# Cached values in earlier places, and the samples' softmax behind the prompt's first two logits steps

## The reference

```python
q, k, v, qi, ki, wi = split(x @ w_in)          # 16 heads of 64, 4 KV heads; 8 index heads
score = einsum(relu(qi . ki), wi) * IDX_SCALE  # every query against every visible key
_, idx = top_k(score, topk)                    # 128 keys (prompt), 256 keys (sample)
logits = q . k_sel * ATTN_SCALE + t5_bias      # only the kept keys
out = softmax(logits) @ v_sel                  # samples: K and V come from paged caches
y = LN(ALPHA * x + out @ w_out)                # then a squared-ReLU MLP, LN, layer 1, MLP
```

## Time and profile before

| what | us |
|---|---|
| median of three runs | 1305.32 |
| lowest and highest run | 1297.4, 1305.51 |
| the profiled execution | 1300.45 |
| its span in the trace | 1298.8 |
| TensorE busy, share of the span | 1215.7, 94% |
| VectorE, ScalarE, GpSimd busy | 708.2, 473.8, 102.0 |
| DMA moved | 129.99 MB |

### The profile page before, as it was taken

How to read it: one execution, slowest core, us unless ns; L and a number is a source line. 1 busy time by engine, 2 the same in 40 slices (tenths; PEclk the granted TensorE clock), 3 DMA queues, 4 the chain that set the end, 5 groups by cost and what they waited for, 6 DMA issues and landing times.

```text
span 1298.8 us, 25590 instructions
## 1 busy us (share of the span) xinstructions
PE 1215.7 (94%) x9573; PEld 1113.3 (86%) x9573; DVE 708.2 (55%) x1440; ACT 473.8 (36%) x863; POOL 102.0 (8%) x139
## 2 busy tenths in 40 slices
PE   8999866999999999999999897889999999999995
PEld 4948723569999999999999896579999999999995
DVE  2289963766764343343357915957833433433477
ACT  2342214763452232231234426744531322322332
POOL 4333430000004000000000210000000000000000
PEclk9989968999999999999999998999999999999998
DMA  6645696002122222222223231012122222222221
GB/s 199 188 144 179 227 288 197 2 1 98 66 66 87 92 97 82 97 97 81 97 88 124 57 97 50 33 50 98 50 98 86 92 98 81 97 96 82 97 82 66
DMA packets 62155, 129.99 MB, mean 100 GB/s; under 512 B 9995, under 2 KB 34483, under 8 KB 61954
## 3 DMA queue, kind: packets, MB, share of 16 engines
q1 hardware_dynamic: 40978, 107.15, 24.3%
q10 hardware_dynamic: 14944, 13.91, 3.5%
q0 software_dynamic: 6160, 7.94, 2.2%
HBM read 124.35 MB, written 9.79 MB: 103 GB/s over the span
## 4 chain that ended last, share of the span: by engine, by line
PE 75%; DVE 16%; ACT 3%; SPq 3%; issue 3%; DMA 1%; POOL 0%; ACTq 0%; DVEq 0%
PE PS L541 59%; PE PS L571 6%; PE PS L761 2%; PE PS L721 2%; PE PS L708 2%; PE PS L735 2%; DVE YA L1521 2%; SPq L371 1%; DVE PB L1657 1%; SPq L362 1%; DVE YA L1508 1%; DVE PB L1682 1%; DVE RSTD L1513 1%; ACT PB L1133 1%; DVE X L1527 1%
## 5 line engine op out<-in xcount | busy, mean ns | idle before, releaser
L1364 DVE TENSOR_TENSOR WLO<-WRAW,WHI 128x1024 fp32r<-128x1024 f32 x118 | 145.3, 1232 | 352.5 <-ACT WHI L966 352.4
L966 ACT ACTIVATE WHI<-WRAW 128x1024 fp32r<-128x1024 f32 x126 | 133.5, 1060 | 404.2 <-PE PS L541 385.7
L541 PE MATMUL PS<-XH,WHI 128*128 128x260 f32 x1344 | 273.1, 284 | 1.9 <-DVE XL L1689 1.6
L541 PE MATMUL PS<-XH,WLO 128*128 128x260 f32 x1344 | 271.4, 284 | 0.0
L541 PE MATMUL PS<-XL,WHI 128*128 128x260 f32 x1344 | 270.8, 283 | 0.0
L541 PEld LDWEIGHTS PS<-XH,WHI 128*128 128x128 f32 x1344 | 207.7, 189 | 3.3 <-DVE XL L1689 2.3
L541 PEld LDWEIGHTS PS<-XH,WLO 128*128 128x128 f32 x1344 | 207.8, 189 | 0.0
L541 PEld LDWEIGHTS PS<-XL,WHI 128*128 128x128 f32 x1344 | 207.2, 189 | 0.0
L541 PE MATMUL PS<-HH,WHI 128*128 128x260 f32 x896 | 181.4, 283 | 0.2 <-DVE HL L1388 0.2
L541 PE MATMUL PS<-HH,WLO 128*128 128x260 f32 x896 | 180.6, 283 | 0.0
L541 PE MATMUL PS<-HL,WHI 128*128 128x260 f32 x896 | 180.3, 283 | 0.0
(11 more groups left out here) (268 smaller groups left out, 1732.1 us busy)
## 6 DMA issues: line engine op xcount, KB each, us to landing
WRAW<-wall SPq DMA_DIRECT2D x168, 512.0 KB, 3.2
bias_skewed<-bias_seq ACTq DMA_DIRECT2D x4, 1280.0 KB, 6.8
BT<-bias_skewed ACTq DMA_DIRECT2D x4, 1024.0 KB, 16.2
X<-xT SPq DMA_DIRECT2D x4, 520.0 KB, 7.2
X<-xT SPq DMA_DIRECT2D x1, 2080.0 KB, 10.2
yT<-X SPq DMA_DIRECT2D x8, 260.0 KB
KVB<-cacheK SPq DMA_DIRECT2D x16, 128.0 KB, 2.7
KVX<-cacheK SPq DMA_DIRECT2D x16, 128.0 KB, 3.0
```

The source lines that it names most:

```text
L541: mm = pe.matmul(PS[:, 2 * slot + g, 0:TG], w[:, slot, k, :], x[:, k, TG * g:TG * g + TG], start=(k == 0 and w is WHI and x is hi), stop=( ...
L966: nc.scalar.activation(WHI[:, slot], WRAW[:, slot], ACT.Copy).then_inc(hi_done, 1)
L1364: V.tensor_tensor(WLO[:, slot], WRAW[:, slot], WHI[:, slot].bitcast(F32), ALU.subtract).then_inc(lo_dve, 1)
```

## The change

What it does, in the order of the program:

- **Places.** `KV_PLACE` gets three new places: 12 (`KVU`, on the first quarter of `UQ`), 13 (a fourth sample in `KVR`) and 14 (`KVZ`, on `KID`, `KIT` and `DS`). The masks `MK` leave `UQ` for `MK0`, `MK12`, `MK3`. V sample 8 is fetched by ScalarE during units 8 and 9, V sample 13 by SyncE once the samples' mask is made. Six V samples are left to `load_values`, and only one of them (15) waits for a K quad. K sample 2 moves from SyncE to ScalarE, units 6 and 7.
- **Page numbers.** They are read ahead: SyncE reads 32 of them before it fetches units 10 to 15, GpSimd 12 before its low parts, ScalarE 12 before the wait at the head of `u == 10`.
- **Digits.** `SLOT_OF` asks for the first 8 counting steps half a unit later, for the last 3 a whole unit later.
- **Bias.** The 4 `bias_skewed` DMAs move from ScalarE (units 8 to 11) to SyncE, ahead of those page numbers. Quarter 0 of `BT` is issued ahead of the samples' exponent, quarters 1 to 3 behind the V products.
- **Stores.** `kip` and `kis` are issued during unit 3, `vp`, `vs` and `kT` by SyncE behind the load of `X32`.
- **Samples.** The bias product stands before the waits behind unit 13; the queries are copied in two parts, 7 of 8 columns a unit earlier; the samples' logits go to PSUM bank 4 on. `logits(0)` and `logits(1)` of the prompt, their `softmax_in` and `exps` come before the samples' transposes and value products. The new token's values come from `NAT` by a product with a diagonal (`DG`), without 8 small DMAs (`VNEW`). Of the 48 prompt rounds, 5 now stand behind `softmax_in(1)` and 5 in steps 0 to 4 of the prompt's attention.

The core of the diff:

```diff
-KV_PLACE = (9, 10, 7, 8, 0, 1, 2, 3, 4, 5, 6, 9, 10, 7, 8, 11)
-PLACES = 12
+KV_PLACE = (9, 10, 7, 8, 0, 1, 2, 3, 12, 4, 5, 6, 13, 14, 11, 9)
+PLACES = 15
-KV_SPLIT = ((8, 8), (8, 8), (8, 8), (0, 8), (8, 8), (8, 8), (0, 8), (0, 8),
-            (4, 6), (4, 6), (4, 6), (5, 7), (5, 7), (5, 7), (5, 7), (4, 6))
+KV_SPLIT = ((8, 8), (8, 8), (0, 0), (0, 8), (8, 8), (8, 8), (0, 8), (0, 8),
+            (0, 0), (4, 6), (4, 6), (4, 6), (4, 6), (8, 8), (4, 6), (4, 6))
-V_ORDER = (8, 9, 10, 15, 11, 12, 13, 14)
+V_LATE = (9, 10, 11, 12, 14, 15)
-SLOT_OF = (1, 2, 3, 4, 5, 6, 7, 8, 10, 11, 12)
+SLOT_OF = (2, 3, 4, 5, 6, 7, 8, 9, 12, 13, 14)
...
@@ SyncE @@
-            sp.wait_ge(ds_mm, 3)
-            with sp.Fori(0, NPG) as pg:
-                load_page(sp, 2, pg)
+            sp.wait_ge(toe_out, 16)
+            for i0 in range(0, P, 32):
+                sp.dma_start(bass.AP(tensor=bskew.tensor, offset=i0 * (NH * SKEW + 1),
+                                     ap=[[NH * SKEW + 1, 32], [SKEW, NH], [1, 640]]),
+                             bass.AP(tensor=bseq.tensor, offset=0,
+                                     ap=[[0, 32], [640, NH], [1, 640]])).then_inc(toe_skew, 16)
+            numbers = page_numbers(sp, 0, (13,) + V_LATE)
             with sp.Fori(POOL_LO[0] // 2 + 1, POOL_LO[1] // 2) as i:
...
-            load_values(sp, 0)
+            sp.wait_ge(mask_done, 1)
+            sp.wait_ge(is_relu, 3 * IDXH)
+            sp.wait_ge(outs, 16 * 2)
+            load_sample(sp, 0, 13, numbers)
+            load_values(sp, 0, numbers)
...
             sp.dma_start(X32[:], io["xT"]).then_inc(x_back, 16)
+            sp.dma_start(io["vp"], NAT[:, 0:QT, HD + IDXH:NATW]).then_inc(outs, 16)
+            sp.dma_start(io["vs"], NAT[0:DB, 4, HD + IDXH:NATW]).then_inc(outs, 16)
+            sp.wait_ge(ev_act, 6)
+            sp.dma_start(io["kT"], UQ[:, 4:6, :]).then_inc(outs, 16)
...
@@ GpSimd @@
+            numbers = page_numbers(pool, 1, V_LATE)
             for u in range(*POOL_LO):
                 low_part(u, u % 2)
...
@@ TensorE @@
+            pe.wait_ge(ds_ev, 1)
+            for c0, c1 in spans:
+                pe.matmul(PSF[:, 2048 + c0:2048 + c1], TREP[:], ohd[:, c0:c1], start=True,
+                          stop=False)
             pe.wait_ge(ev_act, A_OUT)
             pe.wait_ge(qb_ready, 1)
-            pe.wait_ge(is_relu, len(items))
-            for c0, c1 in spans:
-                pe.matmul(PSF[:, c0:c1], TREP[:], ohd[:, c0:c1], start=True, stop=False)
...
@@ ScalarE @@
+                if u == 10:
+                    numbers = page_numbers(act, 2, V_LATE)
                 act.wait_ge(unit_done, u + 1)
                 high_part(u + 2, u % 2)
...
+                if 6 <= u < 10:
+                    with act.Fori(4 * (u % 2), 4 * (u % 2) + 4) as pg:
+                        load_page(act, 2 if u < 8 else DB, pg)
...
+            act.wait_ge(toe_skew, 16 * 4)
+            act.wait_ge(kv_used, DB)
+            load_bias(0)
             act.wait_ge(d_mx, 1)
...
                 if i == -1:
+                    for q in range(2):
+                        act.wait_ge(kv_used, DB + 4 * q + 4)
+                        nc.scalar.activation(OV[:, q, :], PS[0:112, 6 + q, 0:256], ACT.Copy
+                                             ).then_inc(ov_ev, 1)
+                        load_bias(q + 1)
+                    load_bias(3)
+                if i == 0:
                     act.wait_ge(do_mm, 1)
...
@@ VectorE @@
-            prompt_rounds(8)
-            dve.wait_ge(ev_act, A_OUT)
+            prompt_rounds(4)
             dve.wait_ge(z_qb, 2)
...
+            dve.wait_ge(ev_act, A_OUT - 1)
+            queries(0, 7)
+            dve.wait_ge(ev_act, A_OUT)
+            queries(7, 8).then_inc(qb_ready, 1)
+            prompt_rounds(6)
...
-            prompt_rounds(len(left))
+            dve.wait_ge(d_p, 1)
+            V.tensor_scalar(DG[:], ident, PD[:, 1024:1025], None, ALU.mult).then_inc(dg_done, 1)
...
                 if i == -1:
+                    prompt_rounds(5)
+                else:
+                    prompt_rounds(1)
+                if i == 0:
                     dve.wait_ge(do_hi, 1)
```

More of the change, by code:

```diff
@@ L503, in _ @@
                 load_page(pool, 3, pg)
+            numbers = page_numbers(pool, 1, V_LATE)
             for u in range(*POOL_LO):
                 low_part(u, u % 2)
-            pool.wait_ge(nat_ev, 5)
-            pool.wait_ge(unit_done, A_OUT)
-            for b in range(DB):
-                pool.dma_start(VNEW[0:1, b, :], NAT[b:b + 1, 4, HD + IDXH:NATW]
-                               ).then_inc(vnew_in, 16)
-            load_values(pool, 1)
+            load_values(pool, 1, numbers)
             pool.wait_ge(ev_dve, 16)
@@ L698, in logits @@
                             pe.wait_ge(top_p, t + 1)
[L699 to L700 removed]
+                        mask = masks[t].rearrange(
+                            "p (g w) -> p g w", g=1).broadcast_to([P, pairs, w])
                         for e in range(2):
@@ L849, in _ @@
                             if c0 < 1024:
-                                mm = pe.matmul(PSF[r, c0:c0 + 512], q,
+                                mm = pe.matmul(PSF[r, 2048 + c0:2048 + c0 + 512], q,
                                                kv_place(n)[:, c0 // P:c0 // P + 4,
@@ L856, in _ @@
                             else:
-                                mm = pe.matmul(PSF[r, 1024:1025], q,
+                                mm = pe.matmul(PSF[r, 3072:3073], q,
                                                UQ[:, 4 + gp, SEQ + b:SEQ + b + 1],
@@ L871, in _ @@
-            for b in range(DB):
-                pe.matmul(sample_out(b), PNEW[0:1, NH * b:NH * b + NH], VNEW[0:1, b, :],
-                          start=True, stop=False)
-            for quad in (range(0, 4), range(4, 8)):
-                for b in quad:
-                    wait_kv(DB + b)
-                for k in range(NPG):
-                    for b in quad:
-                        mm = pe.matmul(sample_out(b), PTD[:, k, NH * b:NH * b + NH],
-                                       kv_place(DB + b)[:, k, :], start=False,
-                                       stop=(k == NPG - 1))
-                        if k == NPG - 1:
-                            mm.then_inc(kv_used, 1)
+            def sample_out(b):
+                return PS[32 * (b % 4):32 * (b % 4) + NH, 6 + b // 4, 0:256]
@@ new lines, in sample_values @@
+            def sample_values():
+                pe.wait_ge(d_p, 1)
+                for k in range(NPG):
+                    pe.transpose(PS[:, 4 + k // 4, (k % 4) * P:(k % 4 + 1) * P],
+                                 PD[:, k * P:(k + 1) * P], ident)
+                pe.wait_ge(dg_done, 1)
+                pe.matmul(PS[0:DB, 6, 0:P], CST[:, C_SAM:C_SAM + DB], DG[:],
+                          start=True, stop=True).then_inc(dt_mm, 1)
+                pe.wait_ge(dt_ev, 1)
+                for b in range(DB):
+                    pe.matmul(sample_out(b), PNEW[:, NH * b:NH * b + NH],
+                              NAT[0:DB, 4, HD + IDXH:NATW], start=True, stop=False)
+                for quad in (range(0, 4), range(4, 8)):
+                    for b in quad:
+                        wait_kv(DB + b)
+                    for k in range(NPG):
+                        for b in quad:
+                            mm = pe.matmul(sample_out(b), PTD[:, k, NH * b:NH * b + NH],
+                                           kv_place(DB + b)[:, k, :], start=False,
+                                           stop=(k == NPG - 1))
+                            if k == NPG - 1:
+                                mm.then_inc(kv_used, 1)
```

126 lines of the change are left out of this document (55 added, 71 removed).

## The result

| | us |
|---|---|
| kernel before, 20 runs beside the changed one | 1301.14 median (1297.4 to 1305.51) |
| changed kernel, 20 runs | 1306.75 median (1304.48 to 1309.53) |
| ratio | 1.0043, 95% interval 1.0032 to 1.0054 |
| span in the profile, before and after | 1298.8 and 1303.4 |

The change costs 0.4%: 5.6 us, where 10 to 14 us of gain were forecast. That is within 1% of before, but a loss: the interval lies above 1.

A forecast was written before the change was run, and what follows sets the result against it. TensorE held 75% of the chain; only its waits, mostly for V, could be won. Gain 20.9 at the first turn less 9.6 in steps 0 to 5, 11.3 us: 1289.1 by profile, 1294.0 by median, said 1291, range 1279 to 1305.

The forecast's parts named there:

- Step 1: Units 10 to 13 get weights later behind page numbers: unit 10 starts +3.8 us, unit 13 ends at 163.7, +7.0 us.
- Rival (c): Four skewing DMAs fill SyncE's queue, which loses 18.8 us; unit 10 starts at 152.8; 1308 by profile; chance 0.1.
- Step 2: Unit 13 to the samples' probabilities: VectorE bounds, rounds end at 175.4, probabilities at 179.7 against 178.6 before.
- Step 3: Values and bias: quarter 0 issued at 174.5, landed at 184.5; first turn at 198.0, 20.9 us earlier.
- Step 4: Steps 0 to 5 of the prompt's attention: 28.0 us instead of 18.4, 9.6 more; step 5 normalised at 226.0.
- rival (b): ScalarE's queue blocks in issues of bias quarters, holding ScalarE to 210; gain about 1, 1299; chance 0.15.
- rival (a): Late weights cost nothing, all of the +7.0 us comes back; gain 18.3, called 1284; chance 0.2.

The follow-up runs named there:

- The first experiment: Changed kernel with page numbers spread over SyncE's, GpSimd's and ScalarE's units instead of read in one piece: 1301.54 us, ratio 1.0015 to the kernel before.
- The experiment with the quarters first: Changed kernel with SyncE waiting for bias quarter 3 before fetching units 16 and 17, loading X32 and sending the stores: 1298.36 us, ratio 0.998.
- Q: Theory that bias quarters behind X32 hold ScalarE in their issues; tested on the changed kernel by SyncE waiting for the last quarter: 1298.36 us.

## Why the prediction was wrong

**Step 1, the fetch of unit 10** was forecast at 126.4 and came at 129.73. The 32 numbers took what was said (111.5 to 129.73, 18.2 us); the four issues were sized at 2.16 us and took 4.82, the last of them 2.77. The landing then was right by luck: 3.2 us behind the issue. The first experiment shows that the account was wrong in kind: the time of that fetch did not matter, since the 5.2 MB of skewing ahead of it on the same queue held the weights until 132.9 even with the fetch out at 112.3. In the changed kernel both limits fall together; either one alone delays unit 10 (cast at 132.91 with the skewing alone, at 128.17 with the numbers alone, at 118.54 with neither). Rival (c) named the right transfers with the wrong mechanism: SyncE was not blocked for 18.8 us in issuing, its weights were late in landing. The line of the prediction that each skewing DMA "took 6.8 us to land when alone" was no price for four back to back, 10.2 to 22.1 us here. The Trainium skill says on the same page as cited before (DMA: Bandwidth & Descriptors, Queues, rings and completion order) that on each DMA engine the descriptors of a queue are consumed in ring order; the trace agrees with that, with the two landings at 132.9 and 133.0, and I had used that section only for sharing between queues.

**Step 1, unit 12 and unit 13.** ScalarE's 12 numbers held the cast of unit 12 as described (cast at 150.76, `issue` as the releaser), and its low part ended at 154.3, 2.7 later than the forecast start of 151.6. Nearly all of that is the cast of unit 10, 2.6 later than forecast (133.01 against 130.4). Unit 13 ended at 167.5, 3.8 later than forecast; the other 1.1 lies between the two starts, where the second digit of unit 12 waits until 158.18 for VectorE, and the three digits were sized at 0.6. The clock cost nothing, as taken: the slow stretch lies ahead of the wait for unit 12, which covers it, and from 144 to 168 the granted clock is 1.00.

**Step 2** put the maximum at 175.4, and it came at 181.91: 3.8 from step 1, 2.7 its own. VectorE was not the bound, as forecast; the row's releaser is TensorE's K logits, which ran at the 1.2 GHz level (granted clock 0.50 from 172 to 176), and I had taken 2 us off for a faster clock that did not come. They also began later than said: the last query copy ended 4.1 us behind unit 13 (171.55), where 2.5 were allowed.

**Step 3.** Quarter 0 took 11.9 us where 10 were allowed, 0.6 beyond the longer of the two bounds given, and went out at 181.75 instead of 174.5, with the last use of a K sample. The first turn came at 207.1 instead of 198.0. 6.5 of these 9.1 us are the lateness that the maximum shows too. Here the step was right in its mechanism: `softmax_in(0)` is released by a quarter, five rounds follow, and the first turn is 11.8 us earlier than before.

**Step 4 is the step that failed.** It had quarter 1 issued at 191.5, landed at 199.5, and "against" rival (b) that only the third quarter would wait. Quarter 1 was issued at 200.05 and landed after 16.0 us, at 216; quarter 2's issue stood for 10.56 us, quarter 3's for 4.65, and ScalarE was held to 215.9, 6 us beyond the 210 that (b) allowed. The transfers do take turns, as rival (b) had it, but turn by packet and not by byte: from 206 to 208, SyncE's queue and ScalarE's have 33 packets each, with 0.55 MB and 0.02 MB in them (the last section shows the rows). So beside `X32` a quarter all but stands still. Step 5 was normalised at 244.2 instead of 226.0: of these 18.2 us, 9.1 were there at the first turn and 9.1 are this step's. The experiment with the quarters first gives back 8.4. I gave (b) 0.15 although had its price: 7.467 us for one issue. The timeline of ScalarE before shows it fuller still: two issues took 13.81 us.

```profile
180.96 4.79 ACTq L1252 DMA_DIRECT2D BT<-bias_skewed  x2
185.78 13.81 ACTq L1252 DMA_DIRECT2D BT<-bias_skewed  x2
199.63 0.38 ACT L1268 ACTIVATE OV<-PS 112x256 f32<-112x256 f32 x1 [17.57 <-issue]
```

The same block stood in the kernel before, where the V products (to 204.8) covered it. The change took that cover away and moved the issues to where the first turn waits for ScalarE. What stands in the earlier trace rows as a median of 5.2 us was the price of a wait that happened to be free.

**The sum.** A gain of 11.3 us became a loss of 5.6. The experiments give 8.4 us to Q, 5.2 to the numbers and 4.4 (alone) to 9.3 (behind the others) to the skewing, 22.4 together; of these the forecast had charged 7.0, in step 1. By steps, the end of step 5 is 18.2 us later than forecast: 3.8 in step 1, 2.7 in step 2, 2.6 in step 3 and 9.1 in step 4. Without the three costs the kernel takes 1284.3, 6.7 below the forecast of 1291 and at the time that rival (a) gave for late weights that cost nothing; its first turn, at 191.9, is also where the steps put it without the 7.0 (198.0 less 7.0). The size of the idea itself was right, and its three side costs were not. A time within 1%, which had 0.43, is what came. The 0.10 for a loss of over 1% was that of (c), whose own price of 7.5 us is 0.6% and so lies within 1%. The range, 1279 to 1305, missed by 1.75 us: its upper end stood between (b), at 1299, and (c), at 1308, and it never took two of the cases together, such as the blocked queue with weights later than step 1 had them.

## What to carry to other kernels

A DMA issue that takes several us in the trace is a blocked engine, even where nothing waits for that engine; before moving it, ask what will then stand behind it, and whether the transfers beside it on the other queues (here `X32` and two units) can go later. Ahead of a fetch on the same queue, count the bytes that have not landed, not only the issues: 17.5 us of earlier issue bought nothing behind 5.2 MB of skewing. And where two repairs share a chain, price them together as well: undone in the changed kernel, the reordering seemed worth nothing that could be told from no change, and it was worth 8.1 us once the queue was clear.

## What was unexpected of the hardware

- Three quarters in 512-byte rows, alone on the DMA engines, run at about 290 GB/s: 3.15 MB, with 12.9 us from the first issue to the last packet (198.82 to 211.7), and with issues that take 1.65 and 3.97 us. Beside `X32`, two units and the stores, the same three need 22.6 us (200.05 to 222.6), while the total stays near 310 GB/s. Packets, MB and share of the 16 DMA engines' time by queue, q1 being SyncE's and q10 ScalarE's, in the changed kernel from 206 to 208:

```profile
q1 hardware_dynamic: 33, 0.55, 89.5%
q10 hardware_dynamic: 33, 0.02, 2.8%
```

  From 206 to 212, when smaller rows follow on SyncE's queue:

```profile
q1 hardware_dynamic: 673, 1.63, 78.6%
q10 hardware_dynamic: 676, 0.35, 19.2%
```

  And with the quarters first, from 198 to 213:

```profile
q10 hardware_dynamic: 6192, 3.15, 81.6%
```

  The two queues have the same number of packets in each of these stretches of the changed kernel, whatever is in a packet: 0.55 MB in 33 is some 17 KB each, and the quarters' packets have about 0.5 KB each. The Trainium skill's rule that an engine takes turns between queues packet by packet (same page and section) agrees with it. It means that a transfer in small rows all but stops beside one in very large rows.
- The issue of a third quarter ends when the first of the three lands: 215.90 and 216.05 in the changed kernel, 205.06 and 205.12 with the quarters first. So a long issue here shows how late an earlier transfer is.
- A skewing DMA (1.28 MB within DRAM) landed after 6.8 us when issued once per unit, and after 10.2 to 22.1 us when four went out within 5 us; and other transfers of the same queue that were issued behind them came late with them: with the skewing DMAs alone moved, the pages of sample 2 landed after 8.4 us (median) instead of 2.0.
